# Level products of the recurrent scan by head on row halves, their keys weighed on GpSimd

## What is computed

```
def step(state, inp):
    qt, kt, vt, bt = inp                       # bt: running sum of log decays
    diff = bt[:, :, :, None, :] - bt[:, :, None, :, :]
    decay = jnp.where(lower, jnp.exp(jnp.where(lower, diff, 0.0)), 0.0)
    scores = jnp.einsum('bhtk,bhsk,bhtsk->bhts', qt, kt, decay)
    o = (jnp.einsum('bhts,bhsv->bhtv', scores, vt)
         + jnp.einsum('bhtk,bhkv->bhtv', qt * jnp.exp(bt), state))
```

## Time and profile before

| | us |
|---|---|
| median of 3 runs | 3423.84 |
| lowest, highest | 3414.9, 3428.85 |
| profiled execution | 3424.76 |
| its span, first to last instruction | 3422.7 |
| PE busy | 3270.0 (96%) |
| first scan, POOL's first queries to the last merge | 2060.45 to 2166.9 |
| second scan, the same | 2865.10 to 2973.3 |

### The profile page before, as it was taken

The page is one execution under the profiler, slowest core; times in us unless marked ns, Lnnn a source line. Parts: engine busy times, 40 slices in busy tenths (PEclk is TensorE's granted clock), DMA queues, the critical chain, the costliest instruction groups (busy, mean ns, idle before and its releaser), DMA issues. The chain is left out here.

```text
span 3422.7 us, 44858 instructions
## 1 busy us (share of the span) xinstructions
PE 3270.0 (96%) x16138; PEld 2504.5 (73%) x16138; DVE 2080.9 (61%) x3509; ACT 968.0 (28%) x2213; POOL 1569.0 (46%) x1534
## 2 busy tenths in 40 slices
PE   7989999999999999999999978999999988999998
PEld 5666555555556967888888945688888865688887
DVE  7567756544444387455555668488764776656554
ACT  2066211001021165211122256322212236432211
POOL 1054323222235424544454548465645547755554
PEclk9999999999999999999999999999999998999999
DMA  7300223333312110344432200244443210022222
GB/s 251 125 23 2 99 86 123 117 117 105 123 57 65 66 38 14 105 158 165 157 124 85 85 20 14 77 149 156 156 150 102 88 46 16 20 92 87 87 87 80
DMA packets 91131, 317.88 MB, mean 93 GB/s; under 512 B 10817, under 2 KB 13153, under 8 KB 90913
## 3 DMA queue, kind: packets, MB, share of 16 engines
q1 hardware_dynamic: 64224, 218.34, 19.7%
q10 hardware_dynamic: 24768, 90.19, 7.2%
q0 software_dynamic: 1920, 6.49, 0.7%
HBM read 312.88 MB, written 2.10 MB: 92 GB/s over the span
## 5 line engine op out<-in xcount | busy, mean ns | idle before, releaser
L1354 PE MATMUL ps<-arena 128*128 128x256 f32 (+1 forms) x3744 | 952.4, 408 | 0.2
L1354 PEld LDWEIGHTS ps<-arena 128*128 128x128 f32 x3744 | 710.8, 190 | 205.0 <-issue 1.7
L2792 POOL TENSOR_TENSOR arena<-ring,arena 128x512 f32<-128x512 f32 (+1 forms) x140 | 181.6, 1297 | 837.0 <-PE ps L1354 837.0
L1354 PE MATMUL ps<-arena,ring 128*128 128x256 f32 (+1 forms) x2032 | 525.1, 410 | 3.1 <-ACT arena L1708 3.1
L1354 PE MATMUL ps<-hbuf,ring 128*128 128x256 f32 (+1 forms) x1824 | 471.6, 409 | 5.0 <-ACT hbuf L1815 2.0
L1354 PEld LDWEIGHTS ps<-arena,ring 128*128 128x128 f32 x2032 | 385.3, 190 | 119.8 <-ACT arena L1708 6.3
L1354 PEld LDWEIGHTS ps<-hbuf,ring 128*128 128x128 f32 x1824 | 349.0, 193 | 113.3 <-ACT hbuf L1815 16.2
L2330 DVE TENSOR_TENSOR arena<-ps,arena 128x256 f32<-128x256 f32 (+1 forms) x192 | 86.0, 448 | 357.0 <-PE ps L1354 235.9
L2217 DVE CUSTOM_DVE_ANT_0 aring<-aring,csil,adab 128x1024 f32<-128x1024 f32 x176 | 261.8, 1508 | 1.7
L2335 DVE SCALAR_TENSOR_TENSOR resid<-ps,mod,resid 128x256 f32<-128x256 f32 (+2 forms) x296 | 137.4, 482 | 185.4 <-PE ps L1354 180.3
L2775 POOL TENSOR_TENSOR arena<-ring 128x512 f32<-128x512 f32 (+1 forms) x140 | 181.2, 1294 | 141.3 <-PE ps L1354 133.2
(11 more groups left out here) (327 smaller groups left out, 5209.3 us busy)
## 6 DMA issues: line engine op xcount, KB each, us to landing
aring<-in_ada ACTq DMA_DIRECT2D x172, 512.0 KB, 4.7
ring<-in_mlp SPq DMA_DIRECT2D x128, 512.0 KB, 3.8
ring<-in_up SPq DMA_DIRECT2D x88, 512.0 KB, 3.3
ring<-in_in SPq DMA_DIRECT2D x56, 512.0 KB, 3.3
ring<-in_down SPq DMA_DIRECT2D x32, 512.0 KB, 3.6
ring<-in_odd_in SPq DMA_DIRECT2D x24, 512.0 KB, 3.2
arena<-in_ada SPq DMA_DIRECT2D x16, 512.0 KB, 13.8
ring<-in_out SPq DMA_DIRECT2D x16, 512.0 KB, 3.2
```

Of the source, the lines that this page charges most:

```text
L1354: return nc.tensor.matmul(ps[:, bank, 0:p.tw], w, x, start=start, stop=stop, skip_group_check=True)
L2792: nc.gpsimd.tensor_tensor(s[3], f0[:, h:2 * h], s[1], ALU.subtract).then_inc(wsum_ready, 1)
```

## The change

- `level_queries`: 16 buffers of 128 x 256 instead of eight of 128 x 512. Both heads lie in the same columns, head 0 in rows 0 to 63, head 1 in rows 64 to 127. No zeros are needed, and the four memsets go.
- POOL: one multiplication of 128 x 256 for the queries of a level instead of four of 64 x 128, and in front of it one more of 128 x 256 for the keys. DVE's `weigh_levels`, and the semaphore level_weighed, go.
- PE: eight matmuls a level, each on 64 rows and 64 moving columns, head by head, instead of four on 128 rows and 128 columns; 16 records instead of 8.
- PSUM: each head has its own bank, so two levels are in flight instead of four. Level li waits from li = 2 on until level li - 2 is taken. The wait of the first pair product for taken levels is one level later than before.

```
-            k = v % 8
-            return (X, H)[k // 4][:, 2 * (k % 4):2 * (k % 4) + 2, S:T]
+            k = v % 16
+            return (X, H)[k // 8][:, k % 8, S:T]
...
-        def level_bank(v):
-            return (v % 7 + 1) % 4
+        def level_bank(v, hx):
+            return 2 * ((v % 7 + 1) % 2) + hx
...
-                                pe.wait_ge(level_taken, 14 * blk + 7 * d - 2)
+                                pe.wait_ge(level_taken, 14 * blk + 7 * d - 1)
...
                             if li == 0:
-                                pe.wait_ge(level_weighed, 2 * blk + d + 1)
                                 pe.wait_ge(pair_taken, pair_index(blk, d, 1, 3) + 1)
-                            if li >= 4:
-                                pe.wait_ge(level_taken, v - 3)
+                            if li >= 2:
+                                pe.wait_ge(level_taken, v - 1)
                             for t in range(4):
-                                mm = nc.tensor.matmul(ps[:, level_bank(v), t * P:(t + 1) * P], WL[:, 7 * (1 - d) + li, t * P:(t + 1) * P],
-                                                      level_queries(v)[:, t // 2, t % 2 * P:(t % 2 + 1) * P], start=True, stop=True)
+                                for hx in range(2):
+                                    rows = slice(64 * hx, 64 * hx + 64)
+                                    mm = nc.tensor.matmul(ps[:, level_bank(v, hx), 64 * t:64 * t + 64],
+                                                          WL[rows, 7 * (1 - d) + li, t * P:(t + 1) * P],
+                                                          level_queries(v)[rows, 64 * t:64 * t + 64], start=True, stop=True)
...
-                weigh_levels(0)
...
-                    weigh_levels(u + 1)
...
                         for li, m in enumerate(LEVELS):
-                            if v >= 8:
-                                pool.wait_ge(level_ready, v - 7)
+                            if v >= 16:
+                                pool.wait_ge(level_ready, v - 15)
...
-                            for hx in range(2):
-                                rows = slice(64 * hx, 64 * hx + 64)
-                                for half in range(2):
-                                    x = nc.gpsimd.tensor_tensor(dst[rows, half, hx], w[rows, 2 * half:2 * half + 2],
-                                                                q[rows, 2 * half:2 * half + 2], ALU.mult)
-                            x.then_inc(query_ready, 1)
+                            dst = level_queries(v).rearrange("p (t b m) -> p t b m", t=4, m=m)
+                            wk = WL[:, 7 * (1 - d) + li, :].rearrange("p (t b x m) -> p t x b m", t=4, x=2, m=m)[:, :, d]
+                            k = KR[:, 3 * d + b, :].rearrange("p (t b x m) -> p t x b m", t=4, x=2, m=m)[:, :, d]
+                            nc.gpsimd.tensor_tensor(wk, wk, k, ALU.mult)
+                            nc.gpsimd.tensor_tensor(dst, w, q, ALU.mult).then_inc(query_ready, 1)
...
-                    for half in (X, H):
-                        spare = half[:, :, S:T].rearrange("p k (c h v) -> p k h c v", c=2, h=2)
-                        nc.gpsimd.memset(spare[0:64, :, 1], 0.0)
-                        nc.gpsimd.memset(spare[64:P, :, 0], 0.0).then_inc(pool_step, 1)
```

More of the change, by code:

```diff
@@ L514, in build @@
         level_decay = sem("level_decay")
-        level_weighed = sem("level_weighed")
         sums_copied = sem("sums_copied")
@@ L1926, in take_levels @@
                                 t0 = 2 * m * k + m * (1 - d)
-                                from_ = ps[s0:s0 + m, level_bank(v), :].rearrange("p (t h x) -> p h t x", t=4, h=2)[:, hx, :, k * m:(k + 1) * m]
+                                from_ = ps[s0:s0 + m, level_bank(v, hx), 0:256].rearrange("p (t x) -> p t x", t=4)[:, :, k * m:(k + 1) * m]
                                 x = nc.scalar.activation(diagonal(hx)[s0:s0 + m, :, t0:t0 + m], from_, ACT.Copy)
@@ L2631, in weigh_ends @@
                     nc.vector.tensor_tensor(QF[:, d, :], QF[:, d, :], QR[:, b, :], ALU.mult).then_inc(ends_weighed, 1)
[L2633 to L2643, removed]
                 def merge(blk, d):
@@ L2659, in merge @@
                             dst = diagonal(hx).rearrange("p t (b x m) -> p t x b m", x=2, m=m)[:, :, 1 - d]
-                            src = ps[:, level_bank(v), :].rearrange("p (t h b m) -> p h t b m", t=4, h=2, m=m)[:, hx]
+                            src = ps[:, level_bank(v, hx), 0:256].rearrange("p (t b m) -> p t b m", t=4, m=m)
                             x = nc.vector.copy_predicated(dst, mask, src)
@@ L2952, in queries @@
                             v = 42 * n + 7 * u + li
-                            if v >= 8:
-                                pool.wait_ge(level_ready, v - 7)
+                            if v >= 16:
+                                pool.wait_ge(level_ready, v - 15)
                             w = WL[:, 7 * (1 - d) + li, :].rearrange("p (t b x m) -> p t x b m", t=4, x=2, m=m)[:, :, 1 - d]
                             q = QR[:, b, :].rearrange("p (t b x m) -> p t x b m", t=4, x=2, m=m)[:, :, 1 - d]
-                            dst = level_queries(v).rearrange("p a (c h b m) -> p a h c b m", c=2, h=2, m=m)
-                            for hx in range(2):
-                                rows = slice(64 * hx, 64 * hx + 64)
-                                for half in range(2):
-                                    x = nc.gpsimd.tensor_tensor(dst[rows, half, hx], w[rows, 2 * half:2 * half + 2],
-                                                                q[rows, 2 * half:2 * half + 2], ALU.mult)
-                            x.then_inc(query_ready, 1)
+                            dst = level_queries(v).rearrange("p (t b m) -> p t b m", t=4, m=m)
[3 more added lines that the diff above has]
+                            nc.gpsimd.tensor_tensor(dst, w, q, ALU.mult).then_inc(query_ready, 1)
                     def roots(blk, level):
@@ L2997, in add_early @@
                             pool.wait_ge(early_added, KT * n + m + 1)
-                    for half in (X, H):
-                        spare = half[:, :, S:T].rearrange("p k (c h v) -> p k h c v", c=2, h=2)
-                        nc.gpsimd.memset(spare[0:64, :, 1], 0.0)
-                        nc.gpsimd.memset(spare[64:P, :, 0], 0.0).then_inc(pool_step, 1)
-                        steps[0] += 1
-                        pool.wait_ge(pool_step, steps[0])
                     add_early(EARLY_AT[0, "ends"], 42 * n)
```

## The result

The changed kernel took **3451.05 us** (median of 4 runs, 3448.78 to 3454.99) against 3423.28 of the kernel before (4 runs): 1.0084 times as long, 95% interval 1.0062 to 1.0107. Forecast were 3412.0 in a range of 3403 to 3424. It is slower, by 28 us.

The account below looks back on a forecast made before the run. POOL was taken to bound each scan's first block and a chain of PE, ACT and DVE the later ones; 5.6 + 5.9 - 1.0 + 2.0 - 2.0 + 2.3 = 12.8 us off 3424.76 gave 3412.0, range 3403 to 3424.

Parts of the forecast that it names:

- The clock term: Later blocks of both scans: half of the 4.6 us lost to a lowered clock returns, +2.3 us, ends 0 and 4.6.
- The step on PE's part: Level products: 16 half-height records at 0.057 us, set by weight loads, 0.91 us a level as now, no change.
- serial row halves: Rival: row halves don't run side by side at 64 columns, 0.112 us a record, 3467 us; chance 0.08.
- PE's records come at 0.08 or more: Sign that the forecast is wrong: level product records on PE at 0.08 us or more, where 0.05 to 0.06 was expected.
- Blocks 0: First block of each scan: gains of 5.6 and 5.9 us from shorter POOL work, less 1.0 for half clock in unit 0.
- Banks: Two levels in flight instead of four: DVE waits some 0.25 us a unit in eight units, -2.0 us, at worst -5.
- DVE's part: Block 1 of each scan: without the keys, exponents come 4.4 us sooner and unit 3 merges 1.0 us earlier, +2.0 in all.
- The price of a POOL multiplication: POOL's new 128 x 256 multiplications: 0.65 us each, from a 676 ns row, bounds 0.6 and 1.04.
- the factor that the prediction turned down: The skill's rule that two-input elementwise work takes POOL about twice DVE's time, which would make a new multiplication about 1.26 us.
- The two minima: Later blocks at full clock: chain lengths of 36.6 us (block 1) and 35.5 us (block 2), not to get shorter.
- block 2 of the second scan no shorter than 35: Sign for the forecast: that block, 35.4 us at full clock, is at its minimum already and stays at 35 us or more.
- The 12.8 us: Sum of all terms, taken from the profiled execution of 3424.76 us to give 3412.0.

Follow-up runs that it names:

- e1: The changed kernel with 128 moving columns instead of 64 in token tiles 0 to 2: 3418.17 us against 3424.03 before, ratio 0.9982.
- e3: The kernel before with two levels in flight instead of four (two banks in turn): 3427.81 us, ratio 1.0014.
- e5: The changed kernel with 128 moving columns in token tiles 0 to 2 and the keys weighed on DVE again: 3425.88 us, ratio 0.9998.
- e9: The changed kernel, unedited, run again on another chip beside the kernel before: 3453.86 us, ratio 1.0089.
- e10: The kernel of e1, unedited, run again on another chip beside the kernel before: 3416.56 us, ratio 0.9985.

## Why the prediction was wrong

**The clock term failed.** It was put as 4.6 us lost before, "some of it returns", half taken, "with 0 and 4.6 as ends". A further loss was outside both ends. I had asked only for how long PE waits ahead of the slow places. Two rows of the kernel before speak against that already: the values product was slow behind a wait of 0.86 us and fast behind one of 2.23.

```profile
2897.40 5.96 PE L1279 MATMUL ps<-arena 128*64 128x512 f32 x16 [0.86 <-DVE arena L2661]
...
2937.90 3.65 PE L1279 MATMUL ps<-arena 128*64 128x512 f32 x16 [2.23 <-DVE arena L2661]
```

The runs show that the width of the products decides it too. The six blocks of the changed kernel are 31.4 us longer than those of e1 (238.9 - 207.5; by medians on one chip 37.3), and e1 has the clock nearly whole. Against the 4.6 us that were lost before, the term is about -27 us, an estimate, instead of +2.3. The step on PE's part went by the pace of a record alone, "I take no change". That was right of the pace (0.06 us at full clock) and missed what half the columns do to the clock. None of my rivals had this mechanism: the one on the slow side, serial row halves, gives the same 0.11 us a record, but e1 has the same halves at 0.06, so it fell. The sign "PE's records come at 0.08 or more" was there in parts of the changed kernel, by the clock and not by the halves.

The other steps are read from e1, where the clock stands at 1.00 in five blocks of six.

**Blocks 0.** Forecast +5.6 and +5.9 and -1.0, measured 31.85 - 28.91 = 2.9 and 32.20 - 30.47 = 1.7. POOL's multiplications came every 0.69 us at best, not 0.65, and beside DVE's `weigh_ends` they took up to 1.28:

```profile
2059.45 1.17 POOL L2949 TENSOR_TENSOR resid<-arena 128x256 f32<-128x256 f32 x1
2060.58 1.28 POOL L2948 TENSOR_TENSOR arena<-arena 128x256 f32<-128x256 f32 x1
2061.82 0.83 POOL L2949 TENSOR_TENSOR resid<-arena 128x256 f32<-128x256 f32 x1
...
2064.23 0.73 POOL L2948 TENSOR_TENSOR arena<-arena 128x256 f32<-128x256 f32 x1
```

Unit 0 of POOL took 2057.39 to 2068.40, 11.0 us where 9.1 + 0.5 were counted. DVE suffers as well, which I had in no term: the first multiplication of `weigh_ends` (L2630 before, L2631 in e1) went from 745 to 1689 ns in the mean, 11 us in all. One of them, in unit 1, took 3.91 us:

```profile
2075.12 3.91 DVE L2631 TENSOR_TENSOR arena<-arena 128x512 f32<-128x512 f32 x1
...
L2631 DVE TENSOR_TENSOR arena<-arena 128x512 f32<-128x512 f32 x12 | 20.3, 1689 | 1.4
```

Behind it DVE was late for the merge of unit 1, and PE waited 1.41 us in one piece for a level to be merged, so from levels to merge it was 10.05 us, not 8.65.

**The price of a POOL multiplication.** I had set POOL's 676 ns against DVE's 630 and found no factor of two. But 630 is a mean beside a busy POOL. Where POOL was idle for all but the end, seven of DVE's key multiplications came in 2.44 us, 0.35 each, half of POOL's 0.69 for as many elements:

```profile
2056.81 2.44 DVE L2642 TENSOR_TENSOR arena<-arena 128x256 f32<-128x256 f32 x7 [7.25 <-ACT arena L1887]
```

So the factor that the prediction turned down is in its own trace, and the 1.26 us that it drew from it came of doubling the slowed DVE time. Its 0.65 us was near all the same.

**Banks.** Forecast 0.25 us a unit, -2.0, up to -5; e3 puts it at 4.8 alone (1.7 to 7.9 by its interval), the bad end. What I left out is PE's own end in the even units. In e1 unit 4's levels begin at 2135.89 and unit 5's at 2151.42, 15.5 us, where I had 14.45: PE finishes the levels 8.1 us after their start instead of 6.4, and roots, pair products and `early` follow it without a gap. There PE, not the merge, is last.

**DVE's part.** Forecast +2.0; e5 against e1 gives some 5.5 us for the move of the keys; block 1 of the first scan is 3.2 us longer in e5, in part by the clock. Right in mechanism (unit 3 is merged late when DVE has the keys), and probably too small.

**The two minima.** 36.6 and 35.5 us for later blocks were to hold; e1 took 37.1 and 36.9 to 37.0, with levels to merge in 9.0. The sign "block 2 of the second scan no shorter than 35" held. So with the clock kept the change is worth 5 to 6 us, not 12.8. Of these the return of the clock loss may be up to 4.6, twice what the sum had for it, so the other terms, +10.5 in the sum, are worth only 1 to 3 us there (3424.03 - 3418.17 = 5.9 by medians, 214.7 - 207.5 = 7.2 by blocks, each less 4.6; an estimate).

**A slip in the sum.** The 12.8 us were taken from the profiled execution, 0.9 above the median; from the median the forecast would have been 3411.0. It changes nothing here.

**Open.** Why the clock falls for narrow products is not shown, only that it does, by degrees and together with two levels in flight. That two levels in flight are needed for the loss is shown for the kernel before only: row halves with 64 columns and four levels in flight weren't tried, since a level being written and one being taken would share a bank.

## What to carry to other kernels

Where the weight load sets the pace, fewer moving columns save no time, and here they cost 33 to 37 us by the clock: compare the granted clock of a stretch before and after, not the busy share, and try the wider product even if part of it is thrown away. When a term of a sum is a clock, give it an end on both sides of zero. And price a long two-operand instruction on POOL by what DVE does beside it, and the other way round.

## What was not expected of the hardware

- Products of 64 columns at 0.057 us a record brought the clock down to 1.2 GHz within a level phase with one wait of 0.21 us in it, and 128 columns at the same pace did not (7.13 us for 64 records against 2.00 for 32). In the kernel before it took both 64 columns and two banks to lose 30 us; one alone cost 10 or 5.
- A value product behind such a phase took up to 6.46 us, more than the 5.35 and 5.96 of the kernel before, so it ran for most of its length at 1.2 GHz.
- DVE's first multiplication in `weigh_ends` was 745 ns beside half-height POOL instructions and 1198 and 1689 beside full-height ones, in the changed kernel and in e1 (1167 and 1551 when these two ran again, e9 and e10). What makes the last two differ was not tried.
